# A two-layer encoder trunk on one core: the last third of the second projection placed later, and the first steps of attention rearranged

## What is computed

```
layer 0:  h = rms_norm(x);  proj = h @ w_in_ab        # q, k, v of 8 heads A; latents of 8 heads B; gate
          out_a = dilated window attention (8 heads);  out_b = latent attention (8 heads)
          x = x + rms_norm((concat(out_a, out_b) * silu(gate)) @ w_out_ab)
layer 1:  h = rms_norm(x);  q, k, v, gate = split(h @ w_in_c)
          q, k = rope(rms_norm per head);  16 query heads, 4 key heads, dense attention
          x = x + rms_norm((attention * silu(gate)) @ w_out_c)
```

## Time and profile before

| | |
|---|---|
| median of 3 runs | 2119.86 us (2119.23 to 2123.38) |
| the profiled execution, own time | 2123.5 us |
| its span | 2121.7 us |
| PE busy | 2045.0 us (96%) |
| DVE, ACT, POOL busy | 1290.0, 1123.1, 951.9 us |
| chain that ended last | PE 86%, DVE 8%, ACT 2% |

### The profile page before, as it was taken

One profiled execution on the slowest core, in us unless ns is written; L12 is line 12 of the kernel. 1 busy time (PEld: TensorE's weight loads), 2 busy tenths in 40 slices (PEclk: granted clock), 3 DMA queues, 4 the chain that ended last, 5 costly groups with the idle time before them and its releaser, 6 DMA issues.

```text
span 2121.7 us, 25158 instructions
## 1 busy us (share of the span) xinstructions
PE 2045.0 (96%) x9334; PEld 1629.9 (77%) x9334; DVE 1290.0 (61%) x1922; ACT 1123.1 (53%) x1420; POOL 951.9 (45%) x477
## 2 busy tenths in 40 slices
PE   7999998999999999999997999999999999998997
PEld 5878886788888877777885777887777777775785
DVE  6232145325787667684668677524578877888554
ACT  7142234335666666665455444333577777777431
POOL 1222234334555565556001666523467667666501
PEclk9999999999999999999998999999999999999999
DMA  5133478527555554545335232261323333333434
GB/s 189 46 128 131 150 258 310 144 72 152 121 120 111 123 127 92 115 137 182 103 110 180 85 118 101 100 191 65 83 59 81 72 82 70 82 82 110 167 106 157
DMA packets 167578, 260.29 MB, mean 123 GB/s; under 512 B 75472, under 2 KB 84304, under 8 KB 167456
## 3 DMA queue, kind: packets, MB, share of 16 engines
q1 hardware_dynamic: 167456, 258.68, 42.5%
HBM read 160.72 MB, written 97.91 MB: 122 GB/s over the span
## 4 chain that ended last, share of the span: by engine, by line
PE 86%; DVE 8%; ACT 2%; issue 2%; DMA 1%; POOL 1%; SPq 0%; DVEq 0%; ACTq 0%
PE SA L1855 11%; PE OP L1899 9%; PE OP L481 5%; PE SA L481 5%; PE SM L1954 5%; PE OP L1006 5%; PE SA L1954 5%; PE SM L1781 5%; PE SA L1006 4%; PE OP L1906 4%; PE OS L481 3%; PE OS L1899 2%; PE OS L1006 2%; PE OS L1954 2%; PE SM L1777 2%
## 5 line engine op out<-in xcount | busy, mean ns | idle before, releaser
L2303 POOL TENSOR_TENSOR c_PL<-c_PF,c_PH 128x1024 fp32r<-128x1024 f32 x128 | 309.0, 2419 | 152.9 <-ACT c_PH L2031 81.7
L2303 POOL TENSOR_TENSOR ab_PL<-ab_PF,ab_PH 128x1024 fp32r<-128x1024 f32 (+3 forms) x128 | 266.5, 2085 | 190.3 <-ACT ab_PH L2031 130.7
L2028 ACT ACTIVATE ab_PF<-SA 128x1024 f32<-128x1024 f32 (+3 forms) x160 | 143.6, 897 | 159.9 <-PE SA L1816 86.8
L2108 DVE TENSOR_REDUCE c_MH<-SM 128x1 f32<-128x512 f32 x256 | 171.9, 687 | 76.7 <-PE SM L1781 76.2
L2028 ACT ACTIVATE c_PF<-SA 128x1024 f32<-128x1024 f32 x160 | 164.4, 1027 | 94.0 <-PE SA L1855 93.6
L402 POOL TENSOR_TENSOR e_wl<-e_raw,e_wh 128x1024 fp32r<-128x1024 f32 (+1 forms) x31 | 73.6, 2374 | 200.6 <-ACT e_wh L547 200.6
L2031 ACT ACTIVATE c_PH<-c_PF 128x1024 fp32r<-128x1024 f32 x128 | 135.8, 1061 | 4.1
L1855 PE MATMUL SA<-c_Q,c_KA 128*128 128x512 f32 x320 | 129.4, 404 | 8.7 <-ACT c_PF L2028 8.7
L1781 PE MATMUL SM<-c_KA,c_Q 128*128 128x512 f32 x320 | 127.3, 399 | 4.6 <-DVE c_MH L2108 3.2
L1855 PE MATMUL SA<-c_Q,c_KB 72*128 72x512 f32 x320 | 128.3, 401 | 0.0
L2099 DVE CUSTOM_DVE_ANT_0 ab_BS<-SM,ab_Bhi 128x512 f32<-128x512 f32 (+1 forms) x192 | 85.8, 464 | 62.6 <-PE SM L1777 62.4
(11 more groups left out here) (490 smaller groups left out, 6002.6 us busy)
## 6 DMA issues: line engine op xcount, KB each, us to landing
c_Q<-qC_hi SPq DMA_DIRECT2D x32, 384.0 KB, 4.9
e_raw<-in_w_tiles SPq DMA_DIRECT2D x20, 512.0 KB, 4.0
n_raw<-in_w_tiles SPq DMA_DIRECT2D x18, 512.0 KB, 3.7
e_XF<-in_xT SPq DMA_DIRECT2D x12, 512.0 KB, 10.3
silu_gate<-e_ta SPq DMA_DIRECT2D x24, 256.0 KB, 2.0
ab_Q<-qA_hi SPq DMA_DIRECT2D x16, 384.0 KB, 5.3
ab_G<-silu_gate SPq DMA_DIRECT2D x24, 256.0 KB, 3.2
ab_res<-in_xT SPq DMA_DIRECT2D x24, 256.0 KB, 2.9
```

Of the source, the lines that this page charges most:

```text
L2028: nc.scalar.activation(used(PF[p], h, s), used(SA, h, s), ACT.Exp).then_inc(e_done, 1)
L2108: nc.vector.reduce_max(dst, src, axis=AX_X).then_inc(m_done, 1)
L2303: nc.gpsimd.tensor_tensor(used(PL[p], h, s), used(PF[p], h, s), used(PH[p], h, s).bitcast(F32), ALU.subtract).then_inc(p_lo[0], 1)
```

## The change

In the second projection the gate units of the third chunk (chunk 1) leave the front: units 0 to 3 are the two gate tiles times chunks 2 and 0, units 4 to 6 are the first q tile times chunks 2, 0 and 1, so that unit 6 is the first to need the third chunk, and its `x_square_sum` stands behind unit 7. The two units that left come late, as units 55 and 59, and their two weight tiles are loaded and split a second time there. The weight tiles 2 and 3 are split during the end of the first layer, and tile 4 (the fifth) at step 5 of ACT and 6 of POOL. Head sums come two units behind their unit and not one. DVE evicts units 0 and 1 before the last two low parts of x, and adds the squares of the third chunk in three pieces.

In attention PE no longer waits for the constants before the first `max_unit`, but before the first transpose. DVE sets the ones of buffer 0 one unit later, and spreads bias tables over three units. The ones of buffer 1 are set at the end of steps 6 and 9 (behind `both`). The last gate unit's `sigmoid` and `gated` come at step 3 of attention, in both layers. SP's last `store_gate` stays where it was, in front of the loads of the next heads.

```diff
@@ entry (first projection)
-        gated(NC * KT - 1)
...
-            if kind[n] == "gate":
-                sigmoid(gated_units.index(n))
+            if kind[n] == "gate" and n < N - 1:
+                sigmoid(act, gated_units.index(n))
@@ inner (second projection): tiles and units
-        ("values", u, 2, 512) for u in range(4)] + [("x", 12 + t, 8, D) for t in range(6)]
-    U = [(tiles[t], t, c) for c in ORDER for t in range(2)]
-    U += [(tiles[t], t, c) for t in range(2, 12) for c in range(NC)]
+        ("values", u, 2, 512) for u in range(4)] + [("x", t, 8, D) for t in (12, 13, 14, 15, 16, 10, 17, 11)]
+    EARLY = 4
+    U = [(tiles[t], t, c) for c in ORDER[0:2] for t in range(2)]
+    U += [(tiles[2], 2, c) for c in ORDER] + [(tiles[t], t, c) for t in range(3, 12) for c in range(NC)]
     U += [(("value", i), V0 + 3, i) for i in range(TT // 2)]
-    U += [(late_gates[t], V0 + 4 + t, c) for t in range(6) for c in range(NC)]
+    for t in range(6):
+        if t == 5:
+            U += [(tiles[0], V0 + 9, ORDER[2])]
+        U += [(late_gates[t], V0 + 4 + t + t // 5, c) for c in range(NC)]
+    U += [(tiles[1], V0 + 11, ORDER[2])]
...
-    splits = [[w for w in range(2, len(W)) if max(first_unit[w - 1], last_unit[w - 2] + 1) == n] for n in range(N)]
+    splits = [[w for w in range(2, len(W)) if max(first_unit[w - 1], last_unit[w - 2] + 1 - (w > V0 + 5)) == n]
+              for n in range(N)]
@@ inner: SP and POOL
-        if (period, t) == (3, 0):
-            load(sp, 2)
+        if (period, t) in ((3, 0), (3, 1)):
+            load(sp, 2 + t)
...
-                if 0 < w < len(W) - 2:
+                if 1 < w < len(W) - 2:
                     load(sp, w + 2)
...
-        for w in range(2):
+        for w in range(4):
             low_weights(pool, w)
...
-        for g in range(3):
-            gated(g)
-        low_weights(pool, 2)
-        for g in range(3, 6):
-            gated(g)
-        for n in range(6, N):
+        for g in range(EARLY):
+            gated(pool, g)
+        for n in range(EARLY, N):
+            if n == 6:
+                low_weights(pool, 4)
             for w in splits[n]:
-                low_weights(pool, w)
+                if w > 4:
+                    low_weights(pool, w)
@@ inner: PE
-        if w == 0:
+        if n in (0, 2, 6):
...
-            if i < 2:
-                pe.wait_ge(deviation, NC)
+            if i < 3:
+                pe.wait_ge(deviation, 3 - i % 2)
...
-            if n in (0, 2, 4):
-                x_square_sum(n // 2)
-            if n - 1 in qk and n != v0:
-                head_sums(n - 1)
+            if n in (0, 2, 7):
+                x_square_sum(min(n // 2, 2))
+            if n < v0:
+                for m in {8: (4, 5), 9: (6,), 10: (7,), 11: (8, 9), v0 - 1: (n - 2, n - 1)}.get(n, (n - 2,) if n > 11 else ()):
+                    head_sums(m)
@@ inner: ACT
+            if t in (4, 7):
+                high_weights(act, 2 + t // 7)
...
-        for g in range(3):
-            sigmoid(g)
-        high_weights(act, 2)
-        root(act, 2)
-        for g in range(3, 6):
-            sigmoid(g)
-        for n in range(6, N):
+        for g in range(EARLY):
+            sigmoid(act, g)
+        for n in range(EARLY, N):
+            if n == 5:
+                high_weights(act, 4)
+                root(act, 2)
@@ inner: DVE
             if t == KT + 1:
+                for n in range(2):
+                    evict(dve, n)
                 low_x(dve, 2, 6)
                 low_x(dve, 2, 7)
...
-            evict(n)
-            if n == 2:
-                for k in range(1, KT):
+            if n > 1:
+                evict(dve, n)
+            if n in (1, 2, 3):
+                for k in range(1, KT)[3 * (n - 1):3 * n]:
                     add_square(dve, 2, k)
...
-            if n in (4, 8):
-                prepare(n // 2 - 2)
+            if n in (3, 8):
+                prepare(n // 4)
@@ layer (attention)
-    n_set = 4
+    n_set = 3
...
             if h == 1 and s == 0:
-                pe.wait_ge(late_set, 2)
+                pe.wait_ge(late_set, 3)
...
-            if g == MAX0 and part == 0:
-                pe.wait_ge(const_in, 16 * n_const)
-                pe.wait_ge(const_set, n_set)
...
             if g in (sample_at, prompt_at) and part == 2:
+                pe.wait_ge(const_set, n_set)
                 transpose_max(0, g == prompt_at)
...
+            if g == 3:
+                first.last_sigmoid(act)
...
-        def set_ones(b, sem):
-            nc.vector.memset(KB[b][HD:P, :].bitcast(F32), 1.0).then_inc(sem, 1)
+        def set_ones(b, sem, part):
+            if part == 0:
+                nc.vector.memset(KB[b][HD:P, :].bitcast(F32), 1.0).then_inc(sem, 1)
+                return
             nc.vector.memset(VH[b][:, :, HD:P].bitcast(F32), 1.0).then_inc(sem, 1)
...
-                set_ones(0, const_set)
-                nc.vector.memset(M[:].bitcast(F32), 0.0).then_inc(const_set, 1)
-                dve.wait_ge(const_set, n_set)
+                nc.vector.memset(M[:].bitcast(F32), 0.0).then_inc(late_set, 1)
+                dve.wait_ge(late_set, 1)
                 if NA:
                     bias(0, 0)
                     bias(0, 1)
-                    bias_full(0)
-                    bias(1, 0)
-                    bias(1, 1)
             for u in units_beside(g)[2:]:
                 maximum(0, u)
+            if g == MAX0:
+                set_ones(0, const_set, 0)
+                set_ones(0, const_set, 1)
+            if g == MAX0 and NA:
+                bias_full(0)
+            if g in (MAX0 + 1, MAX0 + 2) and NA:
+                bias(1, g - MAX0 - 1)
...
-        set_ones(1, late_set)
         for g in range(G):
...
                 both(h + 1)
+            if g in (6, 9):
+                set_ones(1, late_set, g // 9)
...
+            if g == 3:
+                first.last_gated(pool)
```

More of the change, by code:

```diff
@@ L156 @@
     gates_stored: Callable
+    last_sigmoid: Callable
+    last_gated: Callable
 @dataclass
@@ L396, in gates_stored, with gated, sigmoid @@
             eng.wait_ge(g_stored[s], 16 * 8)
+    def gated(pool, g):
+        pool.wait_ge(g_sig, g + 1)
+        nc.gpsimd.tensor_tensor(ta[g % 3][:], ta[g % 3][:], tb[g % 3][:], ALU.mult).then_inc(g_mul, 1)
+    def sigmoid(act, g):
+        act.wait_ge(acc_read, gated_units[g] + 1)
+        nc.scalar.activation(tb[g % 3][:], ta[g % 3][:], ACT.Exp, scale=-1.0).then_inc(g_exp, 1)
+        act.wait_ge(g_exp, g + 1)
+        nc.scalar.activation(tb[g % 3][:], tb[g % 3][:], ACT.Ln, bias=ones[:, 0:1]).then_inc(g_log, 1)
+        act.wait_ge(g_log, g + 1)
+        nc.scalar.activation(tb[g % 3][:], tb[g % 3][:], ACT.Exp, scale=-1.0).then_inc(g_sig, 1)
     def gpsimd(pool, between):
@@ L611, in high @@
                 nc.scalar.activation(out, bank(n), ACT.Copy, scale=scale).then_inc(hi_done, 1)
-        def sigmoid(g):
-            act.wait_ge(acc_read, gated_units[g] + 1)
-            nc.scalar.activation(tb[g % 3][:], ta[g % 3][:], ACT.Exp, scale=-1.0).then_inc(g_exp, 1)
-            act.wait_ge(g_exp, g + 1)
-            nc.scalar.activation(tb[g % 3][:], tb[g % 3][:], ACT.Ln, bias=ones[:, 0:1]).then_inc(g_log, 1)
-            act.wait_ge(g_log, g + 1)
-            nc.scalar.activation(tb[g % 3][:], tb[g % 3][:], ACT.Exp, scale=-1.0).then_inc(g_sig, 1)
         nc.scalar.preload_act_table_set("natural_log_exp_and_others")
@@ L948, in low_weights, with gated, sigmoid @@
                                 wh[w % 2][:, 0:width].bitcast(F32), ALU.subtract).then_inc(w_lo, 1)
+    def gated(pool, g):
+        pool.wait_ge(g_sig, g + 1)
+        nc.gpsimd.tensor_tensor(ta[g % 3][:], ta[g % 3][:], tb[g % 3][:], ALU.mult).then_inc(g_mul, 1)
+    def sigmoid(act, g):
+        act.wait_ge(acc_read, gates[g] + 1)
+        nc.scalar.activation(tb[g % 3][:], ta[g % 3][:], ACT.Exp, scale=-1.0).then_inc(g_exp, 1)
+        act.wait_ge(g_exp, g + 1)
+        nc.scalar.activation(tb[g % 3][:], tb[g % 3][:], ACT.Ln, bias=ones[:, 0:1]).then_inc(g_log, 1)
+        act.wait_ge(g_log, g + 1)
+        nc.scalar.activation(tb[g % 3][:], tb[g % 3][:], ACT.Exp, scale=-1.0).then_inc(g_sig, 1)
     def gpsimd_ahead(pool):
-        for w in range(2):
+        for w in range(4):
             low_weights(pool, w)
@@ L1159, in square @@
             wait_count(act, q_sum, i - 1)
-            nc.scalar.activation(tsq[i % 2][:], ta[i % 3][:], ACT.Square).then_inc(q_sq, 1)
+            nc.scalar.activation(tsq[i % 2][:], ta[place_of(i)][:], ACT.Square).then_inc(q_sq, 1)
         def head_scale(n):
@@ L1185, in high @@
                                      ).then_inc(hi_done, 1)
-        def sigmoid(g):
-            act.wait_ge(acc_read, gates[g] + 1)
-            nc.scalar.activation(tb[g % 3][:], ta[g % 3][:], ACT.Exp, scale=-1.0).then_inc(g_exp, 1)
-            act.wait_ge(g_exp, g + 1)
-            nc.scalar.activation(tb[g % 3][:], tb[g % 3][:], ACT.Ln, bias=ones[:, 0:1]).then_inc(g_log, 1)
```

(46 more changed lines are left out.)

65 lines of the change are left out of this document (18 added, 47 removed).

## The result

The changed kernel takes 2109.4 us (median of 5, 2106.64 to 2111.54) against 2119.86 for the kernel before (2119.17 to 2123.38): ratio 0.9948, 95% interval 0.9936 to 0.9959, 10.5 us less where 24 were forecast, and outside the forecast's range. In a second series it was 2108.93, ratio 0.9934 (0.9921 to 0.9948).

A forecast was written before the change was run, and what follows sets the result against it. PE was taken as the bound, busy 2045.0 of 2121.7 us, leaving idle time and half clock to win. Terms summed to -25.0: 2098.5 from the profile, 2094.9 from the median; forecast 2096, range 2087 to 2108, its own 2091 to 2101.

The forecast's parts named there:

- Part 1, the late third: Between the layers: PE's loss around units 4, 5 and the third chunk's square sum goes; -18.4 us.
- Rival B: Between the layers: POOL's low parts hold DVE 4.8 us, square sum waits 5; 2103 to 2106 us, chance 0.09.
- D: Between the layers: DVE's whole chain is slowed, square sum waits 27 us; kernel slower, 2126 us, chance 0.04.
- E: Between the layers: the late third only shifts the wait to unit 6; 2110 to 2119 us, chance 0.05.
- Part 1, the head sums' lag: Second projection: later head sums delay ACT's and POOL's work on tile 5 and second value tile; +0.8 us, 0 to 2.
- Part 2: Two gate units and weight tiles moved late: PE waits for a late tile's low part; +0.4 us.
- Parts 3 and 4: Attention's beginning, first and second layer: less loss beside gate units, -6.3 and -1.5 us; in first steps, -5.9 and -5.1.
- Rival A: First steps of attention: the clock falls all the same, in one layer or both; 2101 to 2106 us, chance 0.20.
- Part 5, the ones: Second head's start, each layer: scores wait for a memset behind `both`, +3.5 us, plus 2.0 of clock; together +11.0.
- Rival C: Second head's start: the wait for the ones does not bite, DVE being ahead of PE; 2085 us, chance 0.07.

The follow-up runs named there:

- the fastest kernel: Changed kernel with third root ahead of tile 4's split, unit 4's head sum inside unit 8, tables behind unit 16, ones in steps 6 and 7: 2092.06 us, ratio 0.9856.

## Why the forecast was wrong, step by step

**Part 1, the late third: right in its gain.** Forecast -18.4; the difference went from -0.5 at 1100 to -19.5 at 1185, 19.0. The low parts, the two evictions ahead of them (1.3 us, which do not quite fit into a pause of 1.16), the additions and the square sum were all in time, and PE had no wait in its units 4 to 7, which with their sum took 22.6 us at full clock. Rivals B, D and E fell with that.

**Part 1, the head sums' lag: the step that failed.** I took "+0.8 for both, from 0 to 2". I had looked at when ACT and POOL would come to tile 5, and not at whether DVE would have the squares ready: a wait of PE for a head sum was in no term. I had also reckoned with "a lag of two". The code has more at the start: the head sum of unit 4 stands behind unit 8, four units on, and those of units 5 to 8 three units on. DVE finishes unit 4 ahead of evicting unit 6, so unit 6 stays in its bank until 1172.33. In the trace the stretch behind 1185 gives back 5.8 us (-19.5 to -13.7): 3.3 of waiting for unit 9's head sum, the rest a slow restart and half clock, save for some 0.6 that is no loss of the lag (in the fastest kernel, with a wait of 0.3 and full clock, the same stretch still gives back 0.9). The causes add: unit 4's head scale comes behind unit 8 only, POOL's tile 4 can hold its multiplication by up to 1.9, DVE makes up only 0.8 a unit (5.57 against 6.35), the tables cost 1.1, and from unit 9 on PE asks one unit sooner. With POOL's operation cut short the wait was 1.4; with the tables moved, and in that profile no hold either, 1.3; with the head scale brought forward 0.9; with the last two edits together 0.3. The expectation that set DVE's 5.6 us against a PE unit of 5.45 left out PE's head sum. Rival B had the mechanism, two-input operations held by POOL, in the wrong place: it looked at the squares, which had slack, and not at the rotation behind them. A half clock stretch near 1337 costs the changed kernel another 1.0 in both its profiles. The second profile of the kernel before has one at 1357 as well, and so have both kernels with the attention part alone, near 1353 and 1358; the first profile of the kernel before has none. So it need not be the change's.

**Part 2: right.** The wait for the late tile's low part is 0.5 us (forecast 0.4).

**Parts 3 and 4, attention's beginning: right mechanism, sizes too large.** Against the profile of before they were nearly as forecast: beside the gates -6.7 and -1.7, in the first steps -4.7 and -4.8 (forecast -6.3, -1.5, -5.9, -5.1); the fifth score came 11.2 and 9.9 us behind the first, where 10.4 and 10.0 were forecast. But timed they are worth 12.5 us (the attention part without the wait for the ones), not 18.8. The prices came from one profile of the kernel before, and its half clocks at 409 and 491 don't come in each execution: the profile of that kernel gives -3.6, -1.7, -1.4 and -4.1 at the same four places against the second profile of the kernel before, 10.8 in all. The timed value lies between that and the 17.9 against the first profile. Rival A asked whether the clock would fall after the change; it did not, at those places. Its reason, that no fall came without a gap near 2 us, does not turn round: near 936 PE waits 2.0 us for the maxima in the kernel before and in the changed one, and behind it the clock is 1.00 in both profiles of the kernel before and 0.57 in the changed kernel. I ought to have asked whether it always fell before.

**Part 5, the ones: right, and closer than its parts.** Forecast +11.0, 7.0 of waiting and 4.0 of clock. Timed it is 11.0 on the attention part alone (0.9993 less 0.9941) and 11.0 to 14.0 on the changed kernel (its two series less 0.9882). In the changed kernel's trace the two places give 11.8: waits of 3.0 and 3.8 where 3.5 each were forecast, and 5.0 of clock and restart, of which the 4.0 was a choice between 0 and 5.1 in each layer. Rival C fell. The rule of the Trainium skill on the shared interface ("GPSIMD Engine Reference", section "Specifications") fits here too: `both` took 1.98 us in the second layer, and ended at 1518.25, beside an operation of POOL's that ended at 1518.23.

**The sum.** With the measured terms the projection comes to -19.0 + 5.8 + 1.0 + 0.5 = -11.7 (timed alone: 0.9947 of 2122.3, -11.2), attention to -12.5 + 11.0 = -1.5 (this is no check, since both terms come from timings of the attention part), together -13.2. The two series of the changed kernel gave -10.5 and -14.0. Of the 11.8 us between this sum and the forecast's -25.0, 5.0 are the lag with its clock, 6.3 the prices of parts 3 and 4, 1.0 the half clock near 1337; 0.1 came on top in part 2 and 0.6 more than forecast was gained between the layers. The 1.3 us that the changed kernel loses near 938 in both its profiles are in no term. That half clock stands in eleven of the sixteen profiles, those of the projection alone and of the attention part alone among them, and in neither of the kernel before; why stays open. The 3.1 us at 92 are no part of the change.

## What to carry to other kernels

When a unit is moved ahead and its follow-up work is delayed, add up that work's cycle on every engine beside it and set it against all that PE does per unit, the small sums included: here 5.57 against 6.35, so a lag shrinks by 0.8 us a unit and no faster. Each hold and each extra operation on the way works against that, and what is left is paid where PE asks for a result sooner than before. A cheap operation that a whole phase waits for must not stand behind the last operation of a step: moving one memset of 0.70 us by two steps was worth 11 to 14 us here. And a loss that consists of half clock has to be priced from more than one profile of the kernel before.

## What was not expected of the hardware

In the two profiles of the changed kernel the half clock falls at the same work, to a few tenths of a us, at every place but one. Four of these places lie behind a wait of PE (3.0 us near 512, 2.0 near 938, 3.3 near 1191, 3.8 near 1519); near 1337 PE had no wait at all, and PEclk was 0.60 from 1337 to 1341. The one place that differs is near 84 us. Behind 24 matmuls of one element each (3.54 us together) and with PE never idle, the same code ran without half clock in four of the sixteen profiles, and with 3.4 or 6.8 us of it in the others.

Between kernels the end differs as well. From the matmul that starts at 1831 in the kernel before, the same work with much the same waits (in each of those I compared, `c_MH` 2.7 to 2.8 us and `c_PF` 2.5 us at the longest) took 276.4 to 279.5 us in sixteen profiles. The long ones have more half clock: PEclk from 1880 to 2000 is 0.99 in the kernel before and 0.93 in the kernel with the attention part alone, which had 279.5 and so gave back 3.0 us there. Which of these lengths comes with which kernel stays open.
